# A dilated attention mixer whose queries are ordered by residue modulo 4, with far groups worked in array quarters

## The reference

```
DSW_GROUPS = ((128, 1), (512, 4), (2048, 16))
...
def dsw_mixer(h, w_qkv, q_gain, k_gain, w_o, rel_bias):
    qkv = (h @ w_qkv).reshape(B, S, 3, G, Hg, HEAD_DIM)
    q = rmsnorm(qkv[:, :, 0], q_gain)
    k = rmsnorm(qkv[:, :, 1], k_gain)
    v = qkv[:, :, 2]
    for g, (window, dilation) in enumerate(DSW_GROUPS):
        o, lse = dsw_group(q[:, :, g].transpose(0, 2, 1, 3), k[:, :, g].transpose(0, 2, 1, 3),
                           v[:, :, g].transpose(0, 2, 1, 3), rel_bias, g * Hg, window, dilation)
...
    wts = jax.nn.softmax(jnp.stack(lses), axis=0)
    o = jnp.einsum('gbhs,gbhsd->bshd', wts, jnp.stack(outs)).reshape(B, S, DSW_OUT_WIDTH)
    return o.astype(h.dtype) @ w_o
```

## Time and profile of the kernel before

| | us |
|---|---|
| median of 3 runs | 881.75 (880.66 to 882.27) |
| the profiled execution | 881.07 |
| its span in the profile | 879.3 |
| PE busy in it | 872.3 |
| DVE busy | 620.3 |
| ACT busy | 491.8 |
| POOL busy | 40.4 |

### The profile page before, as it was taken

The page is one execution under the profiler, slowest core; times in us unless marked ns, Lnnn a source line. Parts: engine busy times, 40 slices in busy tenths (PEclk is TensorE's granted clock), DMA queues, the critical chain, the costliest instruction groups (busy, mean ns, idle before and its releaser), DMA issues.

```text
span 879.3 us, 13709 instructions
## 1 busy us (share of the span) xinstructions
PE 872.3 (99%) x5546; PEld 750.9 (85%) x5546; DVE 620.3 (71%) x1064; ACT 491.8 (56%) x742; POOL 40.4 (5%) x69
## 2 busy tenths in 40 slices
PE   9999999999999999999999999999999999999998
PEld 8887888987888888878999988888777899998886
DVE  5889987989988987776666644466778586664441
ACT  7566836667847654576555533355667565553330
POOL 1700010000000000100000000010000000000000
PEclk9999999999999999999999999999999999999999
DMA  8963254642344678623655556555553386555540
GB/s 300 314 257 106 97 192 149 240 145 97 110 163 160 239 242 226 182 70 131 191 184 187 183 203 193 197 186 189 168 168 120 97 282 195 187 186 192 171 152 25
DMA packets 79454, 155.54 MB, mean 177 GB/s; under 512 B 5644, under 2 KB 7852, under 8 KB 79392
## 3 DMA queue, kind: packets, MB, share of 16 engines
q1 hardware_dynamic: 75200, 142.81, 48.2%
q0 software_dynamic: 4192, 11.86, 5.1%
HBM read 153.55 MB, written 1.11 MB: 176 GB/s over the span
## 4 chain that ended last, share of the span: by engine, by line
PE 90%; ACT 4%; DVE 3%; issue 2%; DMA 1%; ACTq 0%; DVEq 0%
PE ps L810 18%; PE ps L812 17%; PE ps L811 17%; PE ps L841 9%; PE ps L842 9%; PE ps L843 9%; PE ps_mid L758 3%; DVE w_lo L1964 1%; ACT w_hi L1465 1%; PE ps_mid L1004 1%; PE ps L758 1%; PE ps_mid L1034 1%; PE ps_mid L810 1%; ACT y_tok L1599 1%; DMA w_raw<-in_w_in 1%
## 5 line engine op out<-in xcount | busy, mean ns | idle before, releaser
L1964 DVE TENSOR_TENSOR w_lo<-w_raw,w_hi 128x2048 fp32r<-128x2048 f32 x133 | 299.8, 2260 | 143.7 <-ACT w_hi L1465 143.5
L1465 ACT ACTIVATE w_hi<-w_raw 128x2048 fp32r<-128x2048 f32 x133 | 250.9, 1891 | 192.2 <-PE ps L812 141.5
L810 PE MATMUL ps<-w_hi,act_hi 128*128 128x512 f32 (+1 forms) x446 | 177.6, 398 | 1.3 <-ACT area L1485 0.9
L812 PE MATMUL ps<-w_hi,act_lo 128*128 128x512 f32 (+1 forms) x446 | 171.1, 384 | 0.0
L811 PE MATMUL ps<-w_lo,act_hi 128*128 128x512 f32 (+1 forms) x446 | 170.8, 383 | 0.0
L810 PE MATMUL ps<-w_hi,hid 128*128 128x512 f32 x296 | 116.1, 392 | 0.0
L812 PE MATMUL ps<-w_hi,hid 128*128 128x512 f32 x296 | 115.2, 389 | 0.0
L811 PE MATMUL ps<-w_lo,hid 128*128 128x512 f32 x296 | 115.2, 389 | 0.0
L841 PE MATMUL ps<-act_hi,w_hi 128*128 128x256 f32 x384 | 109.9, 286 | 0.0
L843 PE MATMUL ps<-act_hi,w_lo 128*128 128x256 f32 x384 | 107.6, 280 | 0.0
L842 PE MATMUL ps<-act_lo,w_hi 128*128 128x256 f32 x384 | 107.6, 280 | 0.0
(11 more groups left out here) (354 smaller groups left out, 1202.1 us busy)
## 6 DMA issues: line engine op xcount, KB each, us to landing
w_raw<-in_ffn_w SPq DMA_DIRECT2D x64, 1024.0 KB, 5.2
w_raw<-in_w_in SPq DMA_DIRECT2D x21, 1024.0 KB, 6.0
w_raw<-in_a_w_qkv SPq DMA_DIRECT2D x18, 1024.0 KB, 4.8
w_raw<-in_b_w_qkv SPq DMA_DIRECT2D x12, 1024.0 KB, 5.0
w_raw<-in_w_out SPq DMA_DIRECT2D x8, 1024.0 KB, 4.8
w_raw<-in_b_w_o SPq DMA_DIRECT2D x4, 1024.0 KB, 5.0
w_raw<-in_w_in SPq DMA_DIRECT2D x12, 256.0 KB, 5.6
w_raw<-in_w_in SPq DMA_DIRECT2D x4, 512.0 KB, 3.5
```

The costliest lines, as they stand in the source:

```text
L810: pe.matmul(o, ah, wh, start=first, stop=False)
L812: mm = pe.matmul(o, al, wh, start=False, stop=last)
L1465: act.activation(w_hi[:, c % RING, :, 0:n], w_raw[:, c % RAW, :, 0:n], ACT.Copy).then_inc(w_hi_done, 1)
L1964: dve.tensor_tensor(lo, w_raw[:, c % RAW, :, 0:n], hi.bitcast(F), ALU.subtract).then_inc(w_lo_done, 1)
```

## The change

Queries of the mixer are no longer taken in blocks of 128 consecutive tokens, but by residue modulo 4. Four query blocks of 64 tokens (residue 2r+t, r and t in 0, 1) are read with a step of 4 out of the turned q. Block (r, t) of head e goes to partitions 64r to 64r+63 of a bank that belongs to head e and t.

- Scores: the near group takes 8 products per pair, 64 queries against all 256 keys (L1130 of the new kernel). The far groups take 16 products per pair, 64 queries against the 64 keys of the same residue, also read with step 4 (L1136), and write them with a step of 2, the two far groups interleaved. Each product uses a quarter of the array: row half e, column half r. A head has then 2 x 384 logits rather than 768 + 384.
- Softmax, bias and scaling: two operations of 384 columns for each head. The bias of a head comes in 6 DMAs rather than one, from a table laid out anew on the host.
- Transposes: for each pair three groups of four 128x128 transposes (two near, one for the far groups of both heads, whose input has a step of 2), 12 groups rather than 24, each copied out as 512 columns by "a", "d", "a" in turn.
- Outputs: the near group takes 8 products of 128 columns (L1171), the far groups 16 products of 64 rows and 64 columns (L1185), again in quarters: row half t, column half e. The sums of a pair lie in two banks.
- The values of the far groups have to lie in the new token order. `mixed_high` on ACT and `mixed_low` on DVE write reordered copies of act_hi and act_lo (2048 columns each), from which blocks f+7 and f+8 are computed. PE waits for both before f+7. The rows' factors `rstd` go to DRAM and back in the new order with three small DMAs on POOL.
- `dil_high` and `dil_low` put the result back in token order.
- The hand-written order is new: `ahead(4)` and `ahead(5)` between the first scores rather than `ahead(7)`, `softmax(2)` and `softmax(3)` ahead of the two `take(f + 8, ...)`, and scores of pair 2 ahead of the last five dense steps.

The core of the diff:

```
-    PCH0 = [0, 16, 32, 56]
+    PCH0 = [0, 16, 32, 44]
...
         if ph == 2:
-            if u < 2:
-                return "d" if (u, g) == (0, 2) else "a"
-            return "ad"[u % 2] if g < 2 or u // 2 == 3 else "a"
+            return "ada"[u % 3]
...
+                with nc.allow_non_contiguous_dma(reason="one element per partition"):
+                    pool.wait_ge(rstd_done, 1)
+                    pool.dma_start(bass.AP(rstd_row.tensor, 0, [[1, 128], [128, 2]]), rstd[:, 0, :]).then_inc(rstd_out, 16)
+                    pool.wait_ge(rstd_out, 16)
+                    for t in range(2):
+                        pool.dma_start(rstd_mixed[64 * t:64 * t + 64, :], bass.AP(rstd_row.tensor, t, [[4, 64], [2, 2]])).then_inc(rstd_in, 16)
...
-                        src = bass.AP(bias_vec.tensor, u * 384, [[1, 128], [8 * 384, 3], [1, S]])
-                        dst = bias_of(u).rearrange("p (g n) -> p g n", g=3)
+                        for r in range(2):
+                            rows = bias_of(u)[64 * r:64 * r + 64]
+                            near = bass.AP(bias_vec.tensor, u * 1152 + 2 * r, [[4, 64], [1, 2], [1, S]])
+                            pool.dma_start(rows[:, 128:640].rearrange("p (t n) -> p t n", t=2), near).then_inc(bias_in[u % 4], 16)
+                            far = bass.AP(bias_vec.tensor, u * 1152 + 896, [[2, 64], [1, 128]])
+                            for at in (0, 640):
+                                pool.dma_start(rows[:, at:at + 128], far).then_inc(bias_in[u % 4], 16)
...
+                    if b == FIRST["dsw"] + 7 and half == 0 and k == 0:
+                        pe.wait_ge(mixed_hi_done, 1)
+                        pe.wait_ge(mixed_lo_done, 1)
...
+                q = lambda e, g, i: qkv[row(e), p % 2, 512 * g + 256 * (p // 2) + i:512 * g + 256 * (p // 2) + 253 + i:4]
+                k = lambda e, g, i: qkv[row(e), p % 2, 1536 + 512 * g + 256 * (p // 2) + i:1789 + 512 * g + 256 * (p // 2) + i:4]
+                for t in range(2):
+                    for r in range(2):
+                        for e in range(2):
+                            pe.matmul(near_scores(e, t)[row(r)], q(e, 0, 2 * r + t), keys(e), start=True, stop=True)
+                for t in range(2):
+                    for g in (1, 2):
+                        for r in range(2):
+                            for e in range(2):
+                                i = 2 * r + t
+                                mm = pe.matmul(far_scores(e, t, g)[row(r)], q(e, g, i), k(e, g, i), start=True, stop=True)
...
+            def far_scores(e, t, g):
+                at = 255 + g - 256 * t
+                return dil_scores(e, t)[:, at:at + 127:2]
...
+            def dil_transposes(n):
+                p, part = n // 3, n % 3
+                if part < 2:
+                    pe.wait_ge(p_scaled, UNIT0[2] + 2 * p + part + 1)
+                if n >= 2:
+                    turned_out(n - 2)
...
+            def dil_far_output(p):
+                turned_out(3 * p + 2)
+                for g in (1, 2):
+                    for r in range(2):
+                        for t in range(2):
+                            for e in range(2):
+                                c0 = 512 * (6 + g) + 64 * (2 * p + e)
+                                at = 2048 + 512 * t + 128 * p + 64 * r
+                                mm = pe.matmul(ps_mid[64 * e:64 * e + 64, at:at + 64], qkv[64 * t:64 * t + 64, r, c0:c0 + 64],
+                                               pt[64 * t:64 * t + 64, 256 * e + 128 * (g - 1) + 64 * r:256 * e + 128 * (g - 1) + 64 * r + 64],
+                                               start=False, stop=g == 2 and r == 1)
...
                 dil_pair_scores(0)
-                ahead(7)
+                ahead(4)
                 dil_pair_scores(1)
+                ahead(5)
+                dil_pair_scores(2)
                 for _ in rest:
                     pass
...
+            def mixed_high():
+                act.activation(tables_turn[:, 0:2048].rearrange("p (k r i) -> p k r i", r=4, i=64),
+                               act_hi.rearrange("p k (i r) -> p k r i", r=4), ACT.Copy).then_inc(mixed_hi_done, 1)
...
-                    for i, n, at, o in ((0, S, 0, 768), (1, 128, 768, 1152)):
+                    for t in range(2):
+                        ins = dve.tensor_tensor_reduce(out=dil_weights(u)[:, t], in0=dil_scores(u % 2, t),
```

More of the change, by code:

```diff
@@ L1080, in dil_pair_scores @@
                     pe.wait_ge(ttr_done, UNIT0[2] + 2 * p)
-                q = lambda e, g, t: qkv[64 * e:64 * e + 64, t, 512 * g + 128 * p:512 * g + 128 * p + 128]
-                k = lambda e, g, ts: qkv[64 * e:64 * e + 64, ts, 1536 + 512 * g + 128 * p:1536 + 512 * g + 128 * p + 128]
-                for g in range(3):
-                    for e in range(2):
-                        o = dil_scores(e)[0][:, S * g:S * g + S]
-                        mm = pe.matmul(o.rearrange("p (t n) -> p t n", t=2), q(e, g, 1), k(e, g, slice(0, 2)), start=True, stop=True)
-                        if g == 0 and e == 1:
-                            mm.then_inc(shared_bank, 1)
@@ L1089, in dil_pair_scores @@
-                for g in range(3):
-                    for e in range(2):
-                        if g == 2 and e == 0:
-                            pe.wait_ge(shared_bank, p + 1)
-                        mm = pe.matmul(dil_scores(e)[1][:, 128 * g:128 * g + 128], q(e, g, 0), k(e, g, 0), start=True, stop=True)
-                mm.then_inc(s_ready, 2)
-            def part_emptied(u, g):
-                engine, n = emptied_by(2, u, g)
-                pe.wait_ge({"a": pt_a, "d": pt_d}[engine], n)
@@ L1100, in dil_transposes @@
-            def dil_transposes(u, g):
-                if u >= 6 and g == 1:
-                    pe.wait_ge(ttr_done, UNIT0[2] + 8)
-                elif g:
-                    part_emptied(u, 0 if u >= 6 else g - 1)
-                else:
-                    pe.wait_ge(p_scaled, UNIT0[2] + u + 1)
-                    if u >= 2:
-                        part_emptied(u - 2, 2)
-                for i, at in enumerate((768 + 128 * g, S * g, S * g + 128)):
-                    mm = turn(t_bank(2, u, g), 128 * i, dil_weights_turn(u, at))
+                row = lambda e: slice(64 * e, 64 * e + 64)
@@ new lines, in dil_transposes @@
+            def dil_transposes(n):
+                p, part = n // 3, n % 3
+                bank = t_bank(2, n, 0)
+                if part < 2:
+                    pe.wait_ge(p_scaled, UNIT0[2] + 2 * p + part + 1)
+                if n >= 2:
+                    turned_out(n - 2)
+                if part < 2:
+                    for chunk in range(2):
+                        for t in range(2):
+                            mm = turn(bank, 256 * chunk + 128 * t, dil_weights_turn(2 * p + part, 0, t, chunk))
+                else:
+                    for e in range(2):
+                        for g in (1, 2):
+                            mm = turn(bank, 256 * e + 128 * (g - 1), dil_weights_turn(2 * p + e, g, None))
```

301 lines of the change are left out of this document (156 added, 145 removed).

## The result

The changed kernel takes 897.22 us (median of 4 runs, 895.41 to 898.04) against 882.01 for the kernel before on the same chip: a ratio of 1.0162, 95% interval 1.0143 to 1.018. It is 15.2 us slower, and the interval leaves no doubt of it; 876.3 was predicted. The profiled execution has a span of 895.2 us, 15.9 more than that of the kernel before. Of these, 2.9 us are lost by 52 us, 9.8 from there to the mixer's first scores, 1.8 in the mixer and 1.4 behind it.

What follows compares the result with a forecast made beforehand. PE, busy 872.3 of 879.3 us, was taken as the bound. Scores -2.2, transposes -2.6, outputs -3.0, old waits -0.8, new waits +4.3 gave -4.3, a second way -5.0; -4.8 from 881.07 made 876.3 us, range 872.8 to 880.6.

Steps and rivals of the forecast that it cites:

- what has to stay hidden: Mixed copies (DVE about 2.3 us, ACT about 1.9) and bias rows (POOL 3.2 us a head) should hold up nothing.
- New waits: PE waits added in the mixer by the new order, together 4.3 us.
- The wait before the scores of pair 2: PE waits 2.6 us for logits of heads 2 and 3, queued behind exponentials, rounding and split.
- Rival 5: PE's clock drops after standing 2.6 us in the mixer; some 3 us more, 879; chance 0.04.
- The wait of 0.8 before pair 1: PE asks for pair 1's scores at 363.4, logits of heads 0 and 1 are through at 364.1.
- The smaller two: PE waits 0.4 us at the second turned group for ps1, up to 0.5 at the third near group's bank.
- Scores: Mixer scores fall from 2.16 to 1.6 us per pair (near 0.94, far 0.52), saving 2.2 us.
- rivals 1 and 3: Small products: only two overlap, 880.2, chance 0.12; or far quarters don't overlap at all, 886, chance 0.08.
- rival 2: Stepped reads and writes slow far scores; doubling adds 0.5 us a pair, 877.3; chance 0.12 for over +1.
- Transposes: Mixer transposes fall from 72 to 48 at 0.108 us each, saving 2.6 us.
- Outputs: Mixer outputs fall from 9.6 to 6.6 us in all, 1.65 per pair, saving 3.0 us.
- the -4.8: Net change forecast for the whole, taken between two sums, -4.3 and -5.0 us.

Runs made afterwards that it cites:

- no_trip: Changed kernel without the three small DMAs of rstd, far values scaled by factors in the old token order: 886.03 us.
- before_store: Kernel before plus only the store of rstd to DRAM in single elements, without the loads back: 893.42 us against 882.76.
- no_trip_later: no_trip with the weight chunk's split moved behind the work of heads 2 and 3 on ACT and DVE: 881.81 us, 0.9998 against the kernel before.
- residue_folds: Changed kernel with factors by small matmuls, split and table loads later, folds writing queries and far keys by residue: 879.78 us, 0.9976 against the kernel before.
- read_step1: no_trip_later with far scores reading queries and keys from 64 columns in a row (output wrong): far scores 0.58 us against 1.06.
- write_step1: no_trip_later with far scores written to neighbouring PSUM columns (output wrong): 885.2 us, far scores 1.07 us against 1.06.

## Why the prediction was wrong

**What was not in the sum: +11 us.** The prediction lists under "what has to stay hidden" the two copies and the bias rows, and not the three small DMAs of `rstd`. I had read them in the change and given them no price, since they are 2 KB and POOL has time. They cost 10.5 to 11.2 us (`no_trip`), all of it by the store (`before_store`). The sentence "the first scores start at 359.11 as before, since nothing on PE has changed by then" is the step that failed: it looked at PE's instructions, and what came late was PE's data. No row of the kernel before shows a store of single elements; a cost without a row wanted a bound from both sides, and this one was put at nothing, without a word in the prediction.

**New waits, sized 4.3, cost about 7.** They measured 5.1 us, and the half clock behind the longest costs some 1.7 more (an estimate from the products between 387 and 392 us). The wait before the scores of pair 2 was placed rightly and named as the costliest step of the mixer; it measured 4.26 us, not 2.6, by the link left out: the rounding waits for `w_used` too, and the step that frees the ring place, the sixth behind the scores of pair 0, came to stand behind the scores of pair 1 when only four dense steps were left ahead of them. Rival 5 came true besides it, priced at some 3 us there: half clock from 385 to 391 us. `no_trip_later` gets 4.2 us back. The wait of 0.8 before pair 1 didn't come, as the scores ahead were slower (2.04, not 1.6); in `residue_folds`, where they take 1.49, it comes, 0.62. The smaller two (0.4 and 0.5) measured 0.48 and 0.32.

**Scores: -2.2 was -0.5.** Near scores came as said (0.98 for 0.94: quarters overlap, rivals 1 and 3 fall). Far ones took 1.06 and not 0.52; this is rival 2, the doubling by steps, at just the price it named, with the cause in the read alone. The argument set against it there, that a float32 product reads at half the pace and so has time, is refuted; nor do they slow down at half clock (1.08), which fits a limit that does not lie in PE's columns.

**Transposes: -2.6 was about -1.9.** A group of four takes 0.44 to 0.50 us and not 0.43, and 0.69 where it follows scores. That a third of them reads in steps of 2 shows nowhere.

**Outputs: -3.0 held.** 1.03 and 0.62 us make the 1.65.

**Hidden work.** The copy `mixed_high` took 3.99 us on ACT and not 1.9 (a read of SBUF in steps of 4), the one on DVE the 2.2 of a split, and both stayed hidden as said. A head's bias rows cost POOL 3.3 us (3.2 predicted) and no engine waited for them.

```profile
325.25 3.99 ACT L1731 ACTIVATE tables_turn<-act_hi 128x2048 fp32r<-128x2048 f32 x1
```

With the trip and the order repaired, the mixer's stretch is 44.44 us against 48.73 (`no_trip_later`), 4.3 faster: near the -4.8 by luck, for that sum held 4.3 us of waits and this one has 0.8. What the work saves was overrated by some 3.5 us (8.6 in the sum, 5.1 measured), 1.7 of it in the scores and 0.7 in the transposes; about 1 us is not attributed. And the head, which the prediction took as unchanged, gives 2 to 3 us of this back before the mixer begins, of which 1 to 2 are traced to the table loads. That is most of why a mixer 4 us faster made no difference to the whole (0.9998, and at best 0.9984) until the tables and the reads were mended; some tenths more are lost between 52 us and the mixer and behind it.

## What to carry to other kernels

Price every DMA that an edit adds by its pieces and by whom it can hold up, not by its bytes or its issuer: a store of single elements to DRAM can all but stop the weight stream of another queue (27 GB/s for 7 us here), and the permutation across partitions that it served was cheaper as eight tiny products. When dense steps are moved, follow what they release (here a place in the weight ring) as well as what they wait for. Where small products read in steps, lay the operand out in rows at a copy that is made anyway.

## What the runs showed of the hardware

- A store of 256 single float32 from SBUF to DRAM took 9 us to land, and meanwhile the other queue's weight packets of 2048 bytes moved at 27 GB/s, the engines counting as half busy and single packets taking up to 8.9 us (84 ns as a rule); the two loads back, also of single elements, could not be told from nothing (893.10 us with them, 893.42 without).
- Matmul operands in steps of 4 float32 doubled products of 64 columns (33 against 18 ns a record); results in steps of 2 float32 in PSUM cost nothing. At half clock the products in steps kept their pace (1.08 us for 32 records against 1.06), while those of 256 columns beside them took 1.77 us in place of 0.98.
- ACT needs 3.99 us to copy 2048 columns read from SBUF in steps of 4, against 1.92 in a row; DVE took 2.2 us for the same copy in the same steps, no more than for a weight split of 2048 columns in a row (2.29), and ACT reads 512 columns of PSUM in steps of 4 in 0.69 us, like its other takes of 512 columns with a factor.
- After pauses of PE of 2.4, 3.2, 4.3 and 7.4 us (`read_step1`, `write_step1`, and two in the changed kernel) the next stretch ran at 1.2 GHz, for 3 to 6 us; after pauses of 2.2 and 2.3 us (`before_store`, `no_trip_later`) it ran at 2.4 GHz.
